# Transposes and the product with V one query block earlier in the attention pipeline of a hybrid decoder block

## The reference

```python
index_score = jnp.where(causal[None], index_score, -jnp.inf)
_, sel = lax.top_k(index_score, topk)                  # 256 keys per query
scores = jnp.einsum('bqhr,bqkr->bqhk', qa, c_sel).astype(jnp.float32) * scale
scores = jnp.where(valid[:, :, None, :], scores, -jnp.inf)
p = jax.nn.softmax(scores, axis=-1).astype(c_sel.dtype)
return jnp.einsum('bqhk,bqkr->bqhr', p, c_sel)
```

## Time and profile before

| | |
|---|---|
| median of 3 runs | 2714.01 us (2712.62 to 2721.93) |
| profiled execution | 2714.01 us, span 2712.3 us |
| attention stage | from about 570 to 797 us of the span |
| TensorE busy | 2516.3 us (93%) |
| VectorE busy | 1345.0 us (50%) |
| ScalarE busy | 692.9 us (26%) |
| GpSimd busy | 713.4 us (26%) |
| mean granted TensorE clock | 0.964 |

### The profile page before, as it was taken

How to read it: one execution, slowest core, us unless ns; L and a number is a source line. 1 busy time by engine, 2 the same in 40 slices (tenths; PEclk the granted TensorE clock), 3 DMA queues, 4 the chain that set the end, 5 groups by cost and what they waited for, 6 DMA issues and landing times.

```text
span 2712.3 us, 33271 instructions
## 1 busy us (share of the span) xinstructions
PE 2516.3 (93%) x12822; PEld 2063.2 (76%) x12822; DVE 1345.0 (50%) x1910; ACT 692.9 (26%) x1394; POOL 713.4 (26%) x289
## 2 busy tenths in 40 slices
PE   6999999959999979979979879999989999999997
PEld 2866878847778868868869758888968888888885
DVE  1339999964434453553553665554543232322226
ACT  3144121134432322422422421002441112121212
POOL 1110222100012241341331523334423322222220
PEclk9999999979999989989989979999999999999999
DMA  6100342144441011021020044333411111111103
GB/s 243 32 32 32 121 158 93 46 140 159 149 127 47 1 62 48 1 78 32 1 78 32 1 171 155 117 137 103 140 63 47 47 47 49 56 50 46 46 31 124
DMA packets 137371, 212.98 MB, mean 79 GB/s; under 512 B 7381, under 2 KB 109109, under 8 KB 136245
## 3 DMA queue, kind: packets, MB, share of 16 engines
q1 hardware_dynamic: 121840, 162.97, 18.3%
q10 hardware_dynamic: 15428, 48.57, 4.6%
HBM read 169.57 MB, written 41.94 MB: 78 GB/s over the span
## 4 chain that ended last, share of the span: by engine, by line
PE 71%; DVE 12%; issue 10%; ACT 3%; DMA 1%; DVEq 1%; ACTq 0%; SPq 0%
PE ps L566 69%; DVE state L1591 2%; DVE zy L1602 1%; DVE decay L1577 1%; PE ps L771 1%; DVE score L1496 1%; DVE top L1492 1%; DVE y_t L1600 1%; ACT decay L1244 1%; DVE state L1592 1%; DVE y_t L1598 1%; DMA ada<-in_ada_w_dram 0%; DVE score L1434 0%; DMA acts_d<-c_out 0%; DVE y_t L1597 0%
## 5 line engine op out<-in xcount | busy, mean ns | idle before, releaser
L566 PE MATMUL ps<-a_hi,w_hi 128*128 128x512 f32 x1728 | 681.5, 394 | 25.0 <-ACT c_out L1168 10.9
L566 PE MATMUL ps<-a_lo,w_hi 128*128 128x512 f32 x1728 | 677.8, 392 | 0.0
L519 POOL CAST w_hi<-raw 128x2048 fp32r<-128x2048 f32 x90 | 173.9, 1933 | 1674.8 <-PE ps L566 1064.6
L566 PE MATMUL ps<-a_hi,w_lo 128*128 128x512 f32 x1728 | 541.2, 392 | 0.0
L521 POOL TENSOR_TENSOR w_lo<-raw,w_hi 128x2048 fp32r<-128x2048 f32 x90 | 425.5, 4728 | 7.2
L566 PEld LDWEIGHTS ps<-a_hi,w_hi 128*128 128x128 f32 x1728 | 327.7, 190 | 98.2 <-ACT c_out L1168 11.6
L566 PEld LDWEIGHTS ps<-a_lo,w_hi 128*128 128x128 f32 x1728 | 327.7, 190 | 69.5 <-issue 1.3
L566 PEld LDWEIGHTS ps<-a_hi,w_lo 128*128 128x128 f32 x1728 | 327.4, 189 | 68.8
L1694 DVE TENSOR_TENSOR x_tm<-x_tm,ps 128x1024 f32<-128x1024 f32 x120 | 146.5, 1221 | 453.1 <-PE ps L566 453.1
L566 PE MATMUL ps<-w_hi,a_hi 128*128 128x256 f32 (+1 forms) x896 | 256.0, 286 | 7.8 <-DVEq L324 4.5
L566 PE MATMUL ps<-w_lo,a_hi 128*128 128x256 f32 (+1 forms) x896 | 254.4, 284 | 0.0
(11 more groups left out here) (235 smaller groups left out, 3235.4 us busy)
## 6 DMA issues: line engine op xcount, KB each, us to landing
raw<-in_w_in_dram SPq DMA_DIRECT2D x31, 1024.0 KB, 5.0
ada_raw<-in_ada_w_dram SPq DMA_DIRECT2D x16, 1024.0 KB, 5.1
raw<-in_w_up_dram SPq DMA_DIRECT2D x16, 1024.0 KB, 5.4
raw<-in_w_down_dram SPq DMA_DIRECT2D x16, 1024.0 KB, 4.8
gates<-gate_d SPq DMA_DIRECT2D x12, 1024.0 KB, 4.9
act_raw<-acts_d ACTq DMA_DIRECT2D x20, 512.0 KB, 6.1
ada<-in_ada_w_dram SPq DMA_DIRECT2D x8, 1024.0 KB, 20.5
gate_d<-spill ACTq DMA_DIRECT2D x16, 512.0 KB, 2.6
```

The lines of the kernel that those rows point to most:

```text
L519: nc.gpsimd.tensor_copy(hi, src).then_inc(hi_made, 1)
L566: return nc.tensor.matmul(o, a, b, start=start, stop=stop)
```

## The change

Three things move one position earlier on TensorE and ScalarE: the transposes with their copies (block t-2 at position t, where it was t-3), the product with V (positions 6, 10, 14, 18, where it was 7, 11, 15, 19) with the copy and DMA of its output, and the adaLN columns (part t-3, where it was t-4). The prologue before the loop has three positions instead of four, the loop's positions run from 3 to 18. Scores, exponentials and VectorE's order stay.

```diff
-                    if t >= 4:
-                        ada_columns(i, t - 4)
-                    if t >= 7 and t % 4 == 3:
-                        g = (t - 4) // 4
+                    if t >= 3:
+                        ada_columns(i, t - 3)
+                    if t >= 6 and (t - 3) % 4 == 3:
+                        g = (t - 3) // 4
...
-                    if t >= 3 and (t < STEPS + 3 or not last):
-                        b = (t - 3) % NT
-                        pe.wait_ge(p_ready, i * STEPS + (t - 2))
+                    if t >= 2 and (t < STEPS + 2 or not last):
+                        b = (t - 2) % NT
+                        pe.wait_ge(p_ready, i * STEPS + (t - 1))
...
-                                                      prob[(t - 3) % 4][:, k * P:(k + 1) * P], ident[:, :])
+                                                      prob[(t - 2) % 4][:, k * P:(k + 1) * P], ident[:, :])
...
-            attend(0, range(4), 0)
+            attend(0, range(3), 0)
             with pe.Fori(0, NH // 2 - 1) as i:
-                attend(i, range(4, STEPS + 4), 1)
-            attend(NH // 2 - 1, range(4, STEPS + 4), 1, last=True)
+                attend(i, range(3, STEPS + 3), 1)
+            attend(NH // 2 - 1, range(3, STEPS + 3), 1, last=True)
```

More of the change, by code:

```diff
@@ L1139, in attend @@
                         act.dma_start(dst[:, (g % 2) * 512:(g % 2) * 512 + 512], att_o[:, :]).then_inc(att_stored, 16)
-                    if t >= 3 and (t < STEPS + 3 or not last):
-                        b = (t - 3) % NT
-                        g = (t - 3) // 4
+                    if t >= 2 and (t < STEPS + 2 or not last):
+                        b = (t - 2) % NT
+                        g = (t - 2) // 4
                         q0 = (b % 4) * P
```

## The result

| | before | after |
|---|---|---|
| median | 2717.65 us (20 runs, 2710.35 to 2725.19) | 2729.40 us (20 runs, 2719.87 to 2755.35) |
| profiled execution | 2714.01 us, span 2712.3 | 2726.80 us, span 2725.1 |
| ratio after to before | | 1.0070, 95% interval 1.0046 to 1.0095 |

The change made the kernel slower by 0.7% by the ratio in the table. The medians alone are 0.43% apart and the means 0.61%. The forecast was 2717 us with 2710 to 2727 as its range, so it was wrong. The medians hide something more: the times after the change fall in two groups. Fifteen of the 20 lie between 2719.87 and 2735.83 us, five between 2752.44 and 2755.35, and nothing in between. The kernel before has one group.

The account below looks back on a forecast made before the run. TensorE was taken to bound the attention stage. Seven heads +3.2, the last head +0.1 and the start 0 gave +3.3 us on 2714.01: 2717 us, own range 2712 to 2723, overall range 2710 to 2727.

Parts of the forecast that it names:

- What bounds the stage: Attention stage: TensorE bounds it, busy 26.55 of 27 us per stretch, so only its standing still can be won or lost.
- Part (a): Before block 5's transposes in each head: TensorE's wait for a late copy goes, gaining 0.59 us per head.
- Part (b): Before block 6's transposes: a new wait of 1.05 us, their copy queued on ScalarE behind block 7's exponential.
- The sum of +0.46 us per head: Each of seven heads: new wait of 1.05 less old wait of 0.59 us; +3.2 us for the seven.
- Part (c): Last head, no next scores: block 6's transposes wait 1.27 us where block 5's waited 1.16; net +0.1 us.
- Part (d): Start of the stage, block 0's transposes before block 3's scores: between -2.6 and +2.6 us, taken as 0.
- The starting point: Profiled execution of the kernel before, 2714.01 us, also the median of three runs, to which the forecast was added.
- the clock rival: At the new wait, each of seven heads drops to the lower clock once, 1.7 us each: 2729 us; chance 0.12.
- Rival "only the gain": Block 7's exponential holds nothing up, all old waits go: 5.3 us faster, 2709 us; chance 0.12.
- Rival GpSimd: Last head: GpSimd's instructions hold VectorE's normalisation of block 3, TensorE loses up to 4.1 us: 2721 us; chance 0.08.

Follow-up runs that it names:

- `copies_first`: Changed kernel with ScalarE copying transposed banks before the exponential at positions without a product with V; 2711.75 us, ratio 0.9982, repeated 2711.14 us, ratio 0.9983.
- `before_copies_first`: Kernel before with ScalarE copying transposed banks before the exponential at positions without a product with V; 2719.68 us, ratio 1.0014.
- The filled kernels: Changed kernel with an unread 512-column matmul in the new wait: seven heads filled, 2720.91 us, ratio 1.0035; last head's too, 2715.13 us, ratio 0.9996.
- `before_spaced`: Kernel before with a repeated 512-column matmul ahead of each product with V of a second half; 2726.30 us.
- `before_in_step`: Kernel before with a repeated 280-column matmul ahead of each product with V of a second half; 2722.72 us, ratio 1.0028.
- `after_spaced`: Changed kernel with a repeated 512-column matmul ahead of each product with V of a second half; 2749.29 us.
- `copies_first_in_step`: Changed kernel with ScalarE's copies ahead of the exponential, plus one repeated 512-column matmul per head; 2723.28 us.
- `again`: Changed kernel, unaltered, measured again on another chip; 2738.22 us.
- `before_deeper`: Kernel before with three small ScalarE copies (64, 64 and 128 columns) after the att_o DMA of each first half; 2715.69 us, ratio 0.9999.

## Why the prediction was wrong, point by point

- **What bounds the stage** (TensorE; only its standing still counts) held for the waits. It was incomplete: TensorE's speed itself depends on how it stands still.
- **Part (a), the old wait goes:** right. Block 5's transposes start 0.81 us after their columns.
- **Part (b), the new wait of 1.05 us behind the exponential of block 7:** right, 1.04 us. `copies_first` shows the cause: with the copies ahead of the exponential the wait is gone.
- **The sum of +0.46 us per head:** right for what it counts, 27.36 against 26.9 us.
- **Part (c), the last head:** 1.27 forecast; measured 787.30 - (785.14 + 0.81) = 1.35 us. What followed it was not forecast: 10.2 us at the lower clock.
- **Part (d), the start:** the wait for VectorE stayed 2.6 us. Nothing lost that shows.
- **The starting point:** 2714.01 us came from three executions; twenty gave 2717.65. That is 3.6 of the 12 us by which the forecast was missed. With it the forecast would have been 2721, still 8 us short.
- **The failed step is the clock rival's.** I named its place and its cause, a deeper wait among small instructions, and then gave it 0.12 and capped it at 1.7 us for each of seven heads, since the last head of before had stood still for 1.16 us without a fall. Three things were wrong in that. One trace says little on something that differs from execution to execution: with the same wait in the last head, `before_copies_first` had 13.6 us at the lower clock. A slow stretch costs 3.3 us here, not 1.7: it lasts 6.8 us, from the wait through the transposes and columns of blocks 6 and 7. And heads don't fall independently: the upper group's trace has all eight slowed at the same instructions. The filled kernels show the size: with the wait's standing still taken away and everything else left, the ratio is 1.0035, with the last head's too it is 0.9996. So most of the 0.7% is the clock; the 3.3 us of waits that I priced (0.12%) lie within the interval of the last of these. That the rival's own time, 2729, is the median measured is luck: it stood for seven heads slowed by 1.7 us each, and neither profile of the changed kernel shows that. One has two heads slowed, by 3.4 and 5.1 us, the other all eight.
- **Rival "only the gain"** did not occur, as argued: ScalarE's order stood in the way. Changing that order gives it: 2711.75 and 2711.14 against 2709 forecast for it.
- **Rival GpSimd:** in the last head block 3's normalisation was held by the cast and took 1.07 instead of 0.49 us, block 4's was held by the subtraction, 3.20 instead of 0.55. TensorE waited for neither. But in `before_spaced`, `before_in_step`, `after_spaced` and `copies_first_in_step`, where other spacings moved the meeting, it lost 2.3 to 2.9 us to such a held normalisation. The mechanism and its size (up to 4.1 us) were right.
- **The Trainium skill's section "HAM oscillation — how this bites in real kernels"** (of "TensorE: Matmul & The Clock Gate"), which I weighed as agreeing for one head in eight, has waits between bursts of a loop that bring the clock down each time. The trace of the upper group agrees, in eight heads of eight. But the page's waits are for DMAs and last some 3 to 5 us, several times the 1.04 us here, so that the page supports this rival less than I made it do; the runs do.

Left open: why an execution of the changed kernel ends up in one group or the other; what exactly about the surroundings makes 1.0 us harmless in seven heads at the old place and 0.9 us harmful at the new one (at the old place five transposes, a small score block and one set of columns, 1.6 us, lie between the product with V and the wait; at the new one those five transposes and the large scores of block 7 come first, then 2.5 us of columns, six transposes, a small score block and columns); and how often the last head's stretch occurs in the kernel before.

## What to carry to other kernels

A wait on TensorE is priced twice: by its length, and by what it can do to the clock behind it. In the upper group here a wait of 1.04 us took 3.3 us more per head in that way. When a change moves a wait into a stretch where TensorE only has small instructions, in a loop, take a slowed turn as a likely case and not as a rival, and look at the spread of the times before the median. The cure need not be a shorter chain: 0.43 us of useless work in the wait of 1.04 us was enough here, 0.16 us was not, and reordering the engine that is waited for (copies ahead of the exponential) removed the wait altogether.

## What the runs showed of the hardware

- TensorE's clock fell behind a wait of 1.04 us that came once per head of 27 us (`after`, `again`), with 8 single-column matmuls, 6 transposes, a small score block and 8 such matmuls again ahead of it. With 0.6 us at the same place no execution out of 12 was in the slow group, with 0.9 us four out of six. A wait of 1.0 us at another place brought no fall in seven heads of `before_deeper`.
- The times of one program fell in two groups 24 us apart; the trace from the upper group has the slow stretch in all eight heads, that from the lower one in two. The distance of the heads mattered: 27.36 us gave the two groups, 27.79 and 28.22 us gave times of 2737 us and more only (six executions each), where the wait was there; without it 27.34 us brought no upper group.
- In the last head, where no scores of a next head follow the wait, a wait of 1.0 us in the view was followed by 13.6 us at the lower clock in one profile (`before_copies_first`) and by none in another (`before`).
- A VectorE normalisation of 512 columns that began 0.02 us after a GpSimd subtraction took 4.77 us in place of 0.49 (`copies_first_in_step`).
- A repeated float32 matmul of 512 columns costs 0.86 us in steady work, one of 280 columns 0.47.
